# The query and key groups of a convolution: from TensorE transposes to one 16-bit DMA transpose per group

## The reference

```python
u = rms_norm(x, norm_g)
p = u @ w_in
qk, v, o, z_a, ig, fg, xb, z_b = jnp.split(p, SPLIT_AT, axis=-1)
qk = jax.nn.silu(causal_dwconv(qk, qk_conv))     # 4 taps along the tokens, 2048 channels
q, k = jnp.split(qk, 2, axis=-1)
...
h = mlstm_chunkwise(q, k, v, i_pre, log_f)       # uses q, k and the gates ig, fg
...
xc = causal_dwconv(xb, lru_conv_w) + lru_conv_b  # a second convolution, not touched
```

## Time and profile before

| | |
|---|---|
| median of 3 runs | 3304.08 us (3303.72 to 3304.55) |
| the profiled execution's own time | 3302.69 us |
| its span, first to last instruction | 3300.9 us |
| TensorE busy | 3288.0 us, 100% of the span |
| TensorE weight loads busy | 2740.2 us, 83% |
| VectorE busy | 2084.4 us, 63% |
| ScalarE busy | 1672.3 us, 51% |
| GpSimd busy | 172.4 us, 5% |
| granted TensorE clock over the span | 1.00 |
| moved by DMA | 617.34 MB, mean 187 GB/s |

### The profile page before, as it was taken

One profiled execution on the slowest core, in us unless ns is written; L12 is line 12 of the kernel. 1 busy time (PEld: TensorE's weight loads), 2 busy tenths in 40 slices (PEclk: granted clock), 3 DMA queues, 4 the chain that ended last, 5 costly groups with the idle time before them and its releaser, 6 DMA issues.

```text
span 3300.9 us, 39862 instructions
## 1 busy us (share of the span) xinstructions
PE 3288.0 (100%) x15436; PEld 2740.2 (83%) x15436; DVE 2084.4 (63%) x2843; ACT 1672.3 (51%) x2273; POOL 172.4 (5%) x241
## 2 busy tenths in 40 slices
PE   9999999999999999999999999999999999999999
PEld 7888888888888888888888888888888888888887
DVE  6557655756757755657667665665565667757664
ACT  5544444546654444546655454454444545555443
POOL 2000000000000000000000000000000321200000
PEclk9999999999999999999999999999999999999999
DMA  8665665565555565565556555555556555565555
GB/s 272 211 199 174 197 181 182 188 194 174 183 182 179 190 185 180 185 200 174 184 197 224 176 192 181 170 168 181 185 179 191 167 175 177 186 211 185 169 183 172
DMA packets 314620, 617.34 MB, mean 187 GB/s; under 512 B 20988, under 2 KB 23364, under 8 KB 314048
## 3 DMA queue, kind: packets, MB, share of 16 engines
q1 hardware_dynamic: 301808, 581.05, 55.3%
q0 software_dynamic: 10336, 27.45, 2.7%
q10 hardware_dynamic: 2288, 6.30, 0.5%
HBM read 608.10 MB, written 6.62 MB: 186 GB/s over the span
## 4 chain that ended last, share of the span: by engine, by line
PE 99%; DVE 0%; ACT 0%; issue 0%; DMA 0%; SPq 0%; ACTq 0%; DVEq 0%
PE acc L1597 30%; PE acc L1599 30%; PE acc L1598 30%; PE tr L1677 2%; PE nm L1778 1%; PE tr L1660 1%; PE tr L1597 0%; PE tr L1599 0%; PE tr L1598 0%; PE tr L1766 0%; PE sc L1752 0%; PE sc L1743 0%; PE tr L1778 0%; PE sc L1757 0%; PE nm L1720 0%; PE sc L1715 0%
## 5 line engine op out<-in xcount | busy, mean ns | idle before, releaser
L1166 DVE TENSOR_TENSOR weights_lo<-weights_raw,weights_hi 128x1024 fp32r<-128x1024 f32 x1103 | 1343.7, 1228 | 958.4 <-ACT weights_hi L888 954.2
L888 ACT ACTIVATE weights_hi<-weights_raw 128x1024 fp32r<-128x1024 f32 x1103 | 1163.8, 1059 | 1144.4 <-PE acc L1599 1105.0
L1597 PE MATMUL acc<-weights_hi,u_hi 128*128 128x512 f32 x3136 | 1239.4, 395 | 0.0
L1599 PE MATMUL acc<-weights_hi,u_lo 128*128 128x512 f32 x3136 | 1223.0, 390 | 0.0
L1598 PE MATMUL acc<-weights_lo,u_hi 128*128 128x512 f32 x3136 | 1221.5, 390 | 0.0
L1599 PEld LDWEIGHTS acc<-weights_hi,u_lo 128*128 128x128 f32 x3136 | 588.6, 188 | 123.7
L1597 PEld LDWEIGHTS acc<-weights_hi,u_hi 128*128 128x128 f32 x3136 | 589.0, 188 | 122.8 <-issue 4.0
L1598 PEld LDWEIGHTS acc<-weights_lo,u_hi 128*128 128x128 f32 x3136 | 589.3, 188 | 118.6
L1597 PE MATMUL acc<-weights_hi,y_hi 128*128 128x512 f32 x1280 | 502.9, 393 | 1.0 <-DVE y_lo L1170 1.0
L1599 PE MATMUL acc<-weights_hi,y_lo 128*128 128x512 f32 x1280 | 499.2, 390 | 0.0
L1598 PE MATMUL acc<-weights_lo,y_hi 128*128 128x512 f32 x1280 | 498.7, 390 | 0.0
(11 more groups left out here) (264 smaller groups left out, 1873.8 us busy)
## 6 DMA issues: line engine op xcount, KB each, us to landing
weights_raw<-in_w_in_dram SPq DMA_DIRECT2D x384, 512.0 KB, 3.6
weights_raw<-in_w_out_dram SPq DMA_DIRECT2D x256, 512.0 KB, 4.3
weights_raw<-in_a_w_in_dram SPq DMA_DIRECT2D x176, 512.0 KB, 4.2
weights_raw<-in_b_w_in_dram SPq DMA_DIRECT2D x112, 512.0 KB, 3.6
weights_raw<-in_c_w_in_dram SPq DMA_DIRECT2D x112, 512.0 KB, 4.3
weights_raw<-in_w_mem_kv_dram SPq DMA_DIRECT2D x63, 512.0 KB, 4.8
kv_scratch<-work ACTq DMA_DIRECT2D x8, 512.0 KB, 5.6
qk_tiles<-in_w_a_dram POOLq DMA_DIRECT2D x8, 512.0 KB, 4.4
```

The lines of the kernel that those rows point to most:

```text
L888: SC_E.activation(WH[:, b % RING], RAW[:, b % RING], ACT.Copy).then_inc(sem("hi_done"), 1)
L1166: V.tensor_tensor(WL[:, b % RING], RAW[:, b % RING], WH[:, b % RING].bitcast(F32), ALU.subtract).then_inc(sem("lo_done"), 1)
L1597: T.matmul(dst, hi_l, hi_r, start=start, stop=False, **kw)
L1599: return T.matmul(dst, lo_l, hi_r, start=False, stop=stop, **kw)
```

## The change

For the query and key groups the piece `ct` is replaced by two pieces on ScalarE. `apart` (slot E+1) copies the two 16-bit halves of each float of `XT` to separate places of `HALVES`, and issues one DMA transpose from `HALVES` to `TURNED` on ScalarE's queue. `join` (slot E+4) waits for the DMA and interleaves the halves again, into the padded buffer `XP`. The convolution's two pieces move from E+2 and E+3 to E+5 and E+6, and `cqs` from E+4 to E+7. The second convolution keeps its `ct`.

```diff
         for j in range(4):
             cq = pl.chunk(("w_in", l, COL_QK + CH * j, 0), "tok", "u", "cq", need=tiles(xt) if j == 0 else None)
-            pl.piece(pl.here() + 1, "ct", to="cq", at=cq)
+            q = pl.piece(pl.here() + 1, "apart", at=cq)
+            pl.piece(pl.here() + 4, "join", at=q)
             for r in range(2):
-                pl.piece(pl.here() + 2 + r, "conv", to="cq", r=r, l=l, taps=QC + 4 * j)
-            pl.piece(pl.here() + 4, "cqs", j=j)
+                pl.piece(pl.here() + 5 + r, "conv", to="cq", r=r, l=l, taps=QC + 4 * j)
+            pl.piece(pl.here() + 7, "cqs", j=j)
...
+        HALVES = W[:, 4612:5636].bitcast(U16)
+        TURNED = W[:, 12560:13584].bitcast(U16).rearrange("p (b k) -> p b k", k=P)
...
                         wait(act, "cz_pe", last.get("cz"))
+                        wait(act, "half_in", last.get("apart"))
                         for t in range(2):
                             i = SC_E.activation(XT[:, t], acc(p)[:, t], ACT.Copy, scale=RSTD["x"][:, t:t + 1])
...
+                    elif k == "apart":
+                        wait(act, "cq_x", p.at)
+                        wait(act, "mo_out", last.get("mo"))
+                        act.wait_ge(sem("kv_st"), 16 * 8)
+                        act.wait_ge(sem("tb_st"), 16)
+                        wait(act, "half_t", 16 * p.n)
+                        for t in range(2):
+                            i = SC_E.activation(HALVES[:, 2 * CH * t:2 * CH * t + 2 * CH].rearrange("p (s f) -> p s f", s=2),
+                                                XT[:, t].bitcast(U16).rearrange("p (f s) -> p s f", s=2), ACT.Copy)
+                        i.then_inc(sem("half_in"), 1)
+                        wait(act, "half_in", p)
+                        wait(act, "yb_lo", last.get("lry"))
+                        act.dma_start_transpose(TURNED, HALVES).then_inc(sem("half_t"), 16)
+                    elif k == "join":
+                        act.wait_ge(sem("half_t"), 16 * (p.at.n + 1))
+                        wait(act, "cx_c", last.get("cx"))
+                        wait(act, "cq_c", p.n)
+                        for t in range(2):
+                            to = XP[:, :, 3 + P * t:3 + P * t + P].bitcast(U16).rearrange("p f (k s) -> p s f k", s=2)
+                            i = SC_E.activation(to, TURNED[:, 8 * t:8 * t + 8].rearrange("p (s f) k -> p s f k", s=2),
+                                                ACT.Copy)
+                        i.then_inc(sem("half_out"), 1)
...
                     elif k == "conv":
-                        wait(dve, "ct_out", last["ct"])
+                        if p.to == "cx":
+                            wait(dve, "ct_out", last["ct"])
+                        else:
+                            wait(dve, "half_out", last["join"])
```

More of the change, by code:

```diff
@@ L20 @@
 F32R = mybir.dt.float32r
+U16 = mybir.dt.uint16
 ALU = mybir.AluOpType
```

## The result

The change costs 10.2 us. The changed kernel takes 3314.71 us (median of 7 runs, 3312.46 to 3316.84), the kernel before 3304.55 us beside it (7 runs, 3303.44 to 3305.14). The ratio is 1.003, its 95% interval 1.002 to 1.0041, so slower by 0.2 to 0.4%. The forecast was 3327: its direction held, the time lies within its range of 3302 to 3385, and its size is 12 us too large. The profiled execution took 3313.93 us (before: 3302.69), its span is 3312.1.

The account below looks back on a forecast made before the run. TensorE was taken to bound the kernel, with 99% of the chain. From 3302.69 us, - 7.1 for transposes and + 30.6 for standing still gave 3326.2, plus 1.4 to the median 3327.6, forecast as 3327; range 3302 to 3385.

Parts of the forecast that it names:

- Removed: TensorE's 8 transposes a group, 0.89 us in each of 8 groups, go: 7.1 us won.
- The pairs of copies: On ScalarE, apart and join each make two 16-bit copies, taken at 2.0 us a pair.
- The landing D = 8 us: Time for the transposing DMA of 512 KB in 2048 pieces to land, taken as 8 us.
- the ring: ScalarE/VectorE chain from one convolution's end to the next: 18.3 + D, 26.3 us at D = 8, against 21.8 a group.
- The upper bound: Highest landing time considered for the DMA: 2048 pieces at 97 ns over 16 engines, plus 1.6: 14.0 us.
- rule of 8 us for each us: With D from 6 us up, each us of D moves the end by 8 us (four groups, two layers).
- The issue's hold: DMA issue on ScalarE's queue: 0.39 us for a plain transfer; up to 4 us would change nothing.
- The gates: Behind the fourth convolution, gates work delays low parts; TensorE loses 13.4 plus 1.9, 15.3 us a layer in all.
- The weights' queue at nothing: Weights' loads have 10.9 us from issue to use against 3.6 to land, so their slowing was costed at nothing.
- (a): Rival: DMA transfer hidden, D 3.6 to 5.6 us, 3303 to 3310, no change that can be told; chance 0.16.
- (b): Rival: pieces cost like 2 KB packets or copies double, + 48 to + 72 us, 3352 to 3376; chance 0.25.
- (c): Rival: faster, gates' pieces find room on VectorE, D under 4 us, full 7.1 us remain, 3297; chance 0.04.

Follow-up runs that it names:

- kernel with more slots: Changed kernel with join in E+6, convolution in E+7 and E+8, cqs in E+12, gates three slots later; 3295.72 us, ratio 0.9975.
- the tanh behind: Changed kernel with cqs in E+10 instead of E+7, behind the next group's eviction, apart and issue; 3310.59 us, ratio 1.0021.
- kernel with three a layer: Changed kernel with each layer's fourth group transposed by TensorE as before, so three DMA transposes a layer; 3313.39 us, ratio 1.0027.
- kernel with two a group: Changed kernel with each group's DMA transpose made twice, the second issue waiting for the first to land; 3348.23 us, ratio 1.0136.

## Why the prediction was right in direction and too large

**Removed: right.** The kernel with more slots wins 7.2 us of span for the forecast's 7.1.

**The pairs of copies: one right, one a third too small.** `apart` takes 1.99 us for two, `join` 2.60 to 2.64 for the 2.0 forecast: its copies are of the same 128x1024 shape and type, but 1.37 us each against 1.05. That is 0.6 us in each ring.

**The landing D = 8 us: the step that failed.** The trace has 5.3 to 6.9, median 5.7. What counts in the ring is the time from issue to the start of `join`; it was 6.4, 7.3, 7.7 and 5.6 us in the first layer (231.74 - 225.38, 257.16 - 249.90, 283.01 - 275.29, 306.72 - 301.14) and 6.3, 6.6, 6.6 and 6.0 in the second. Against 8 that is 5.1 and 6.6 us less in four groups. The larger `join` takes 2.4 back, and the forecast had the other steps of the ring 3.0 too long in all (6.1 us from a convolution's end to the issue for 6.45, 9.5 from the end of `join` to the convolution's end for 9.9). 5.1 - 2.4 + 3.0 = 5.7, and 6.6 - 2.4 + 3.0 = 7.2: the fourth convolution ended 99.4 and 97.9 us after E, where the forecast had 105.1. These 12.9 us are the error: the forecast had + 23.5, the two profiled executions differ by 11.2, which leaves 12.3. Of the 12.9 the time from issue to `join` makes 11.7 and the other steps 6.0, and the longer `join` takes 4.8 back.

**Why 8 was too much.** The estimate took the 5.5 us of the gates' load, with as many pieces and a quarter of the bytes, and added for bytes and for ScalarE's side. The transpose, with all of the bytes, took 5.7; neither addition was due. The queue's row says why the number of pieces didn't tell: q10 grew by 16640 packets and by 1.3% - 0.5% of 16 engines' span, (0.013 x 3312.1 - 0.005 x 3300.9) x 16 / 16640 = some 25 ns for a packet of 256 bytes. The upper bound had used 97 ns. By the forecast's own rule of 8 us for each us, D = 5.7 gives + 5.1, and `join` 0.6 us longer in eight groups + 4.8: + 9.9, against a measured + 10.2. That this comes so near is luck: `join` started 6.5 us after the issue on average and not 5.7, held back by the splits behind the issue, which adds 6.7 by the same rule, and the other steps, too long in the forecast, take 6.0 off. The rule that the Trainium skill gives (Advanced Engine Details and Errata, X-Bar Transpose (TRN2)), that such transposes are as fast as regular DMAs, comes closer than my D: 5.7 us against the 3.6 of a load of the same size and the 5.1 of ScalarE's own stores of it. With the tanh behind, beside 884 KB of loads, one such transfer took 14.6, which that rule does not give.

**The issue's hold: mis-weighed.** The forecast let up to 4 us of it change nothing, and named "the issue holds ScalarE for over 4 us" as a way to be wrong. It was 3.3 to 4.8 in six of the eight groups. It doesn't lengthen the ring much, since the landing would take its place (issue on SyncE: the same time). But it moves the wait: ScalarE doesn't idle ahead of `join`, 2 us and then 4 to 5, as forecast; TensorE waits for low parts whose splits stand behind the issue, which is a second due time, 12.8 and 13.3 us after a convolution's end (256.67 - 243.83, 282.53 - 269.23), not in the forecast at all. With a hold of 0.4 us it would have been met: with the issue on SyncE TensorE has no wait there, its first is at 270.64. In the changed kernel the gates' due time should cover its cost (by the sums above, no run shows it apart), in the kernel with the fourth group on TensorE it is all of the cost.

**The gates: right.** The forecast had the slot behind `gates_row` start 11.9 us after the fourth convolution's end (105.1 to 117.0). It was 330.67 - 318.83 = 11.8. From there on the sum of a layer is the fourth convolution's end less what TensorE has in hand: (99.4 - 89.8) - 3.56 = 6.0 and (97.9 - 89.8) - 3.56 = 4.5, where 89.8 is the forecast's 105.1 - 15.3. The trace has 6.0 and 4.4.

**The weights' queue at nothing: right for this kernel only.** Here the transfer meets few loads, and no wait of TensorE goes back to one, though the splits of these weights waited 18.0 us for loads, in 9 waits, and 1.9 in one before. With the tanh behind it meets many in five groups of eight and moves its data up to four times slower; there the splits waited 33.0 us for loads, in 19 waits.

**Rivals.** (a), hidden, was nearest in D, and hidden is what the transfer is in the kernel with more slots; here it would have given 3303 to 3310, and the time is 4.7 us above that. (b) is out: neither packets of 97 ns nor copies of twice the price. (c) needed D under 4 us.

## What to carry to other kernels

Cost a step that joins a chain by the whole ring from one turn to the next, and compare it with the slots that a turn has: here 25 us against 21.8, and each us over comes back in each of eight groups. When a piece moves to later slots, look at what stands there already: a fourth convolution put on the gates' slots cost 15 us in two layers, and three slots of room for the gates turned a loss of 0.17% into a gain of 0.25%. A DMA that an engine issues itself is an instruction of that engine; look at its duration before you queue the critical path's splits behind it. And look at what other transfers are issued just behind it: one change of slots here made the same transfer take up to 10.9 us in place of 2.4.

## What the runs showed of the hardware

- The issue of a transposing DMA held ScalarE 3.2 to 6.1 us, that of a plain one 0.39. Every fourth in the queue took 1.33 us instead, in all runs in which ScalarE issued them: the fourth and the eighth of eight, in the kernel with three a layer the first of the second layer, and of the sixteen in the kernel with two a group each fourth. Two kinds took 1.8 us: there the other second issues, which wait for the first transfer to land, and with the tanh behind the third of each layer. Issued by SyncE, on the queue of the weights' loads, all eight took 3.3 to 4.7 us, the fourth of each layer too (4.26 and 4.28). Why is open; it isn't what is queued behind.
- 16-bit copies of 128x1024 elements took 1.05 us where the read steps over every second element (`apart`), and 1.37 where the write does, into the padded rows, and the read is in order (`join`).
- 256-byte packets of a transpose took some 25 ns of a DMA engine each in the changed kernel, and 2048 of them 2.2 to 4.9 us with up to 250 KB of loads beside (all runs), 4.1 beside 582 KB and 6.1 to 10.9 beside 756 to 884 KB.
- After waits of 2.5 us and more for low parts TensorE's granted clock stood at its lower level, 1.2 GHz, for some us. Shorter waits went either way: it fell after one of 1.96 us (issue on SyncE) and one of 2.05 (gates' weights one slot later), and did not after 1.97 (issue on SyncE) and 2.27 (transfer twice). In the changed kernel matmuls that come 0.227 us apart came 0.43 apart from 282.53 on (283.06, 283.49). Windows of the kernel with the last group by TensorE:

```profile
284.00:286.00 2.00, 2.00 (x6) 0.50 0.95 321
286.00:288.00 2.00, 2.00 (x6) 0.50 0.93 341
288.00:290.00 2.00, 2.00 (x9) 0.94 0.84 256
```

At 0.50 for about 6 us TensorE did half the work: 3 us of the 8.9 lost there ahead of the gates. In the changed kernel the clock stayed at the higher level after the waits of 1.73 and 1.56 us (256.67, 330.67). There its fall should have cost nothing, as the gates' wait comes behind it; no run tests that.
